# Two-map attention steps of both layers without the product of constants ahead of their transposes

## What is computed

```
def diff_attn_block(q, k, v, lam):
    s = jnp.einsum('bqhmd,bkhmd->bhmqk', q, k).astype(jnp.float32) * q.shape[-1] ** -0.5
    p = jax.nn.softmax(s, axis=-1)
    pd = p[:, :, 0] - lam * p[:, :, 1]
    return jnp.einsum('bhqk,bkhd->bqhd', pd.astype(v.dtype), v)
```

## The kernel before

```
            def keep_busy(dst):


                pe.matmul(dst[:, 0:256], ones, cst[:, 0:256], start=True, stop=True)
```

## Time and profile before

| | |
|---|---|
| median of 3 runs | 1744.42 us (1739.34 to 1745.04) |
| profiled execution | 1744.36 us |
| its span, first to last instruction | 1742.6 us |
| TensorE busy | 1666.6 us, 96% |
| VectorE busy | 1285.7 us, 74% |
| ScalarE busy | 826.7 us, 47% |
| mean granted TensorE clock | 0.990 |
| "c" steps in L0 | about 165 to 208 us of the span |
| "c" steps in L1 | about 771 to 798 us |

### The profile page before, as it was taken

How to read it: one execution, slowest core, us unless ns; L and a number is a source line. 1 busy time by engine, 2 the same in 40 slices (tenths; PEclk the granted TensorE clock), 3 DMA queues, 4 the chain that set the end, 5 groups by cost and what they waited for, 6 DMA issues and landing times.

```text
span 1742.6 us, 28904 instructions
## 1 busy us (share of the span) xinstructions
PE 1666.6 (96%) x11946; PEld 1487.3 (85%) x11946; DVE 1285.7 (74%) x1777; ACT 826.7 (47%) x1196; POOL 243.3 (14%) x199
## 2 busy tenths in 40 slices
PE   6999989999999999999999999969999999899999
PEld 3897667788788876986999999959999999699999
DVE  4777863887988878857578777797998878657453
ACT  3433762543224333636554546575636444555362
POOL 0323001011001111440310121013000220030000
PEclk9999999999999999999999999989999999999999
DMA  8744002233565458320347566634998956037542
GB/s 304 276 159 169 2 1 97 97 145 115 187 241 203 175 202 311 122 73 2 122 151 272 204 202 244 217 123 172 357 364 323 335 213 240 27 125 287 187 176 73
DMA packets 46578, 317.87 MB, mean 182 GB/s; under 512 B 5232, under 2 KB 6256, under 8 KB 12272
## 3 DMA queue, kind: packets, MB, share of 16 engines
q1 hardware_dynamic: 45936, 312.68, 49.2%
q0 software_dynamic: 512, 3.35, 0.5%
HBM read 314.96 MB, written 1.05 MB: 181 GB/s over the span
## 4 chain that ended last, share of the span: by engine, by line
PE 81%; DVE 11%; ACT 3%; issue 3%; POOL 2%; DMA 1%; DVEq 0%; ACTq 0%
PE PM L1629 22%; PE PM L1630 22%; PE PM L1631 22%; PE PM L1904 2%; DVE wlo L1030 2%; PE PX L1940 1%; DVE acc L1064 1%; PE PX L1602 1%; PE PX L1813 1%; PE PO L1966 1%; PE PX L1870 1%; PE PO L1955 1%; DVE Hlo L1527 1%; PE PM L1713 1%; PE PM L1715 1%
## 5 line engine op out<-in xcount | busy, mean ns | idle before, releaser
L1629 PE MATMUL PM<-Hhi,whi 128*128 128x256 f32 (+1 forms) x1686 | 525.9, 312 | 8.6 <-DVE Hlo L1441 3.0
L1630 PE MATMUL PM<-Hlo,whi 128*128 128x256 f32 (+1 forms) x1686 | 522.1, 310 | 0.0
L1631 PE MATMUL PM<-Hhi,wlo 128*128 128x256 f32 (+1 forms) x1686 | 521.9, 310 | 0.0
L1030 DVE TENSOR_TENSOR wlo<-raw,whi 128x2048 fp32r<-128x2048 f32 (+2 forms) x199 | 438.0, 2201 | 96.7 <-ACT whi L721 96.1
L721 ACT ACTIVATE whi<-raw 128x2048 fp32r<-128x2048 f32 (+3 forms) x204 | 365.5, 1791 | 150.8 <-PE PM L1631 95.1
L1629 PEld LDWEIGHTS PM<-Hhi,whi 128*128 128x128 f32 x1686 | 322.2, 191 | 33.4 <-issue 9.7
L1631 PEld LDWEIGHTS PM<-Hhi,wlo 128*128 128x128 f32 x1686 | 322.4, 191 | 16.5
L1630 PEld LDWEIGHTS PM<-Hlo,whi 128*128 128x128 f32 x1686 | 322.4, 191 | 15.8
L1629 PE MATMUL PM<-Ghi,whi 128*128 128x256 f32 (+1 forms) x864 | 265.2, 307 | 1.7 <-DVE X L1211 1.6
L1631 PE MATMUL PM<-Ghi,wlo 128*128 128x256 f32 (+1 forms) x864 | 263.2, 305 | 0.0
L1630 PE MATMUL PM<-Glo,whi 128*128 128x256 f32 (+1 forms) x864 | 263.2, 305 | 0.0
(11 more groups left out here) (226 smaller groups left out, 2244.8 us busy)
## 6 DMA issues: line engine op xcount, KB each, us to landing
raw<-in_ada SPq DMA_DIRECT2D x104, 1024.0 KB, 4.9
raw<-in_wm SPq DMA_DIRECT2D x93, 1024.0 KB, 5.0
raw<-in_wl SPq DMA_DIRECT2D x68, 1024.0 KB, 4.9
raw<-in_wl SPq DMA_DIRECT2D x32, 704.0 KB, 4.2
raw<-in_wm SPq DMA_DIRECT2D x5, 768.0 KB, 4.4
raw<-in_wm SPq DMA_DIRECT2D x4, 704.0 KB, 4.1
X<-in_x SPq DMA_DIRECT2D x1, 2048.0 KB, 12.0
bias<-in_bias POOLq DMA_DIRECT2D x1, 2048.0 KB, 11.1
```

Of the source, the lines that this page charges most:

```text
L1030: dve.tensor_tensor(wslot(wlo, i, usize(u)), slot_raw(n, usize(u)), wslot(whi, i, usize(u)).bitcast(F32), ALU.subtract)\
L1629: pe.matmul(out, st_hi, mv_hi, start=first, stop=False)
L1630: pe.matmul(out, st_hi, mv_lo, start=False, stop=False)
L1631: return pe.matmul(out, st_lo, mv_hi, start=False, stop=last)
```

## The change

In the two-map steps (kind "c") of L0 and L1 the product of constants is left out. It stays in the "m" steps of the second block. With it `take` for the bank moves behind the wait for `cmb`; banks are handed out in the same order as before.

```
@@ -1925,7 +1925,7 @@
                     if 0 <= m < len(steps):
                         x = steps[m]
                         k, nc_ = x["kind"], x["nk"] // 128
-                        if k != "b":
+                        if k == "m":
                             dst = take(("T", st, m, 0))
                             keep_busy(dst)
                         pe.wait_ge(*at("cmb" if k == "c" else "p", (st, m)))
@@ -1934,7 +1934,7 @@
                         per = len(pieces) // t_banks(x)
                         for b in range(t_banks(x)):
                             key = ("T", st, m, b)
-                            if k == "b" or b:
+                            if k != "m" or b:
                                 dst = take(key)
                             for c in range(per):
                                 ins = pe.transpose(dst[:, c * 128:c * 128 + 128], pieces[b * per + c], ident)
```

## The result

The changed kernel took 1756.82 us in the median of 12 executions, against 1743.42 us for the kernel before in 12. The ratio is 1.0045, with a 95% interval from 1.0024 to 1.0066: slower by 0.2 to 0.7%. The median lies further off than the ratio, because the executions of one program fall into groups.

What follows compares the result with a forecast made beforehand. TensorE was taken as the bound, VectorE close behind and tying with it after the removal. Gains of 4.5 us in L0 and 2.7 in L1 made 7.2: 1744.36 - 7.2 = 1737.2 us, range 1732.0 to 1742.5 us.

Steps and rivals of the forecast that it cites:

- The bound and the sum: TensorE bounds the "c" steps, then ties with VectorE; gains 4.5 us in L0, 2.7 in L1, 7.2 in all.
- T(3), T(4), T(5) and T(6): Starts of the transposes of steps 3 to 6 in L0, forecast 1.19, 1.72, 1.29 and 1.23 us earlier.
- the step itself: A 512-key "c" step on TensorE, start to start: 2.96 us with the product, 2.42 without.
- The gain passed on to the end: Behind the last "c" step nothing absorbs the gain, so the full 7.2 us reach the end.
- The clock: Clock in the "c" steps without the product: expected to stay at 1.00, costed at nothing in the sum.
- the second rival: Clock falls in the "c" stretches: 4.84 us per 512-key step, 2.68 per 256-key step, 1781 us if throughout; chance 0.11.
- the nearest row: "b" steps of L0, without such a product: TensorE idle 3.5 of 51.6 us, clock 1.00; taken as the clock's guide.
- T(1): Start of the transposes of step 1 in L0, forecast to move from 173.04 to 172.87: 0.17 us gained.
- The rule on transposes: Skill's rule that transposes don't engage the full clock, so "c" steps may drop; judged not to bite here.
- The range: Whole kernel's time, 1732.0 to 1742.5 us; left out the clock's fall and the case of no gain.

Runs made afterwards that it cites:

- e1_only_l1: Product removed only in the eight two-map steps of L1, against the kernel before: median 1752.68 us against 1743.63, ratio 1.0041.
- e2_only_l0_512: Product removed only in the eight 512-key steps of L0, against the kernel before: median 1764.67 us, ratio 1.0127.
- e4_split_late: Changed kernel with the first mixer part's split moved behind the two-map steps: median 1755.29 us, against 1743.63 for the kernel before.
- f4_rows32: Kernel before with the product on 32 rows instead of 128 in all 24 two-map steps: median 1740.68 us.

## Why the prediction was wrong

**The bound and the sum** were right in mechanism. Starts in the changed kernel, from the first scores on, show T(3), T(4), T(5) and T(6) moved forward by 1.08, 1.55, 1.14 and 1.09 us; the prediction had 1.19, 1.72, 1.29 and 1.23. The term mis-sized is the step itself: transposes that follow a wait or the scores take 0.49 us up to the values, not 0.44, so a step takes 2.49 us and not 2.42. Where the clock held, L0 gains 3.8 us and not 4.5 (the kernel that keeps 1, 5 and 6, where the product costs L0 nothing; no profile of the changed kernel itself shows a held L0), and L1 gains 2.3 and not 2.7. Two executions of the changed kernel, 1737.4 and 1737.8, are at the forecast of 1737.2. In part that is luck: the gain was put 1.1 us too high, and it was taken from 1744.36, 0.9 above the median of the 12 executions. The gain passed on to the end, as said.

**The clock** is the step that failed: "So I cost the clock at nothing in the sum", and with it the chance of 0.11 for the second rival. The runs showed the rival's mechanism, place and, nearly, its price: 4.65 us per step of 512 keys at half clock (4.84 by the rival) and 2.52 per step of 256 keys (2.68). It comes in part of the stretches only, so the ten executions that fell take 1745 to 1766 us and not 1781. Each us at half clock cost about 0.4 us and not 0.5: in e1_only_l1 13.1 us (65.55 against the held 52.46) for 30.7. Part of the difference is that TensorE's own waits shrink in exchange (at the transposes of step 1 from 0.61 to 0.19 us).

Two readings led there. The first: the "b" steps at 1.00 were taken as the nearest row. They are not so near. Per us they have less idle time (3.5 of 51.6 us, 7%) than the new "c" steps turned out to have (2.8 of 20.4 us, 14%, from 165.0 to 185.4), and their scores use 64 rows, those of "c" 32. The second: only the new waits were weighed. The old one of 0.94 us ahead of the scores of step 2 stood there all along, in the kernel before too. In three lines of that kernel's timeline (the old wait, the scores of a "b" step, the longest wait among the "b" steps):

```profile
169.32 1.13 PE L1904 MATMUL PM<-QT 32*128 32x512 f32 x4 [0.94 <-ACT acc L927]
...
205.39 1.13 PE L1904 MATMUL PM<-QT 64*128 64x512 f32 x4
...
231.78 1.09 PE L1977 MATMUL PX<-cst,T 128*128 128x128 f32 x8 [1.64 <-DVE T L1341]
```

A wait of 1.64 us in the "b" stretch left the clock at 1.00, and 0.94 us did so in the "c" stretch as long as the product stood behind it. So the length of a wait alone does not decide; with the product gone behind the 0.94 us the clock fell in most executions. In three of the four profiles that fell near the start (L1 alone, L0's 512-key steps alone, the product on 32 rows) it fell in the scores of step 3, ahead of T(1). In the fourth (split moved) it fell at the end of the wait at T(1), which the working had as a lost gain only ("T(1) only moves from 173.04 to 172.87").

**The rule on transposes.** The prediction weighed a rule of the Trainium skill (TensorE: Matmul & The Clock Gate, Part 4: PE-mode transpose), that transposes don't count as a busy TensorE the way products do, against the "b" steps. The sign that came out is the rule's, but not by its way: with five float32 transposes in the product's place, which by the rule should protect nothing, ten executions of ten held. On this point the measurement differs from the page and decides.

**The range** left out the rival that came. From one profile of an execution in which the clock held, nothing could tell how near to falling it was; in hindsight a chance of 0.11 was too low for an edit that takes away only work that keeps TensorE busy.

What stays open: why a given execution falls and another doesn't. And whether what counts is the kind of work or the waits. For the waits: six warming products instead of four, which fill the 0.94 us, held in five of five. For the work: a product at step 0, which leaves that wait open, held in ten of ten; 1.64 us of waiting among "b" steps did nothing; and a product on 32 rows fell in three of ten. Both seem to matter, and no run separates them.

## What to carry to other kernels

A product of constants has a price that one profile shows and a use that it does not; take such products away one place at a time, and look at the times and clocks of a dozen executions, not at one. Most of them could go: eight of 24 (steps 0, 1, 5 and 6 of each layer) were enough in ten executions of ten; four of 24 (steps 0 and 1), with the split moved, in five of five, which is too few to rely on. Put them behind the longest wait, or where the engine waits anyway for a step whose combination comes late: there they cost 0.0 us in L0 and 0.3 us in L1. Filling the wait itself worked too.

## What was not expected of the hardware

Once it had fallen, the clock stayed low for 27 to 65 us in the five profiles that fell, in work that kept TensorE busy almost without a gap (27.18 of 27.3 us, 30.51 of 30.7, the other three in full): in e2_only_l0_512 for 54.6 us, 24 of them with the product of constants back in every step. In the kernel before the same steps with the same products ran at 1.00 from the first to the last. So in these traces the same work held the upper level and did not bring it back within 24 us. In all five it came back among the "b" steps (212.7 in the changed kernel, 220.4 in e4_split_late, 228.3 in e2_only_l0_512, 239.2 in f4_rows32, 808.5 in e1_only_l1).

Two products on 32 rows each, scores and constants, were recorded as starting 0.01 us apart at 174.24 and 174.25. This happened in every second 512-key step of f4_rows32 and made the product free there: in L1, at the upper clock, scores and product together took 1.06 us from start to start (812.26 to 813.32), as long as the scores alone. In the steps between they did not overlap, and the product cost 0.43 us (1.49 from 809.35 to 810.84).
